# A two-layer hybrid diffusion step on one Trainium2 core: long convolution by channel halves, modulation items moved, another opening order, filler multiplications around the norms

## What is computed

```python
def trunk_layer(x, cond, p, rope, ctx_k, ctx_v):
    mod = (jax.nn.silu(cond) @ p['mod_w'] + p['mod_b']).reshape(-1, 1, 6 * D)
    sh1, sc1, g1, sh2, sc2, g2 = jnp.split(mod, 6, axis=-1)
    h = rms_norm(x, p['norm1_w']) * (1 + sc1) + sh1
    proj = h @ p['w_in']
    ...
    filt = hyena_filters(L, ...)
    ya = hyena_mixer(hy, p['hy_short_w'], p['hy_short_b'], filt, p['hy_bias'])
    ...
    yb = blocked_gqa(q, keys, vals)
    ...
    merged = (jax.nn.sigmoid(ga) * (ya @ p['w_br_a']) + jax.nn.sigmoid(gb) * (yb @ p['w_br_b'])
              + jax.nn.sigmoid(gc) * (yc @ p['w_br_c']))
    x = x + g1 * (merged @ p['w_o'])
    h2 = rms_norm(x, p['norm2_w']) * (1 + sc2) + sh2
    x = x + g2 * expert_choice_moe(h2, p['router_w'], ...)

def hyena_mixer(hy, short_w, short_b, filt, bias):
    parts = jnp.split(conv3_centred(hy, short_w, short_b), 3, axis=-1)
    z = parts[0]
    for o in range(2):                       # 512 channels, two long convolutions in turn
        z = parts[o + 1] * bidir_fftconv(z, filt[:, 0, o], filt[:, 1, o], bias[o])
    return z
```

## Time and profile before

| | us |
|---|---|
| median of 3 runs | 2371.03 (2369.81 to 2376.42) |
| the profiled execution, its device time | 2374.17 |
| the profiled execution, its span | 2372.5 |
| opening, to the first chunk at full pace | 0 to 206 |
| long convolution, layer 0 | 671.9 to 766.2 |
| long convolution, layer 1 | 1770.7 to 1855.1 |
| second norm and router, layer 0 | 915.8 to 936.5 |
| choice of tokens, layer 0 | 936.5 to 971.1 |

### The profile page before, as it was taken

One profiled execution on the slowest core, in us unless ns is written; L12 is line 12 of the kernel. 1 busy time (PEld: TensorE's weight loads), 2 busy tenths in 40 slices (PEclk: granted clock), 3 DMA queues, 4 the chain that ended last, 5 costly groups with the idle time before them and its releaser, 6 DMA issues.

```text
span 2372.5 us, 38587 instructions
## 1 busy us (share of the span) xinstructions
PE 2204.2 (93%) x14538; PEld 1859.6 (78%) x14538; DVE 1389.1 (59%) x2253; ACT 998.8 (42%) x1780; POOL 167.9 (7%) x221
## 2 busy tenths in 40 slices
PE   7998999999888998699997999999897999599999
PEld 3447999999645996588886999999763898388887
DVE  4756533611766654788887443431358764688887
ACT  2333222222631223588885321222360222488885
POOL 0000000010100100111110000001100110011110
PEclk8999999999999998799998999999998999799999
DMA  9792222233324431899992222233401341599995
GB/s 367 281 335 80 76 85 72 110 119 116 131 114 159 161 103 65 317 383 388 382 389 80 72 78 83 81 122 120 166 22 44 126 136 54 210 387 388 384 377 190
DMA packets 72959, 436.19 MB, mean 184 GB/s; under 512 B 9289, under 2 KB 9929, under 8 KB 31930
## 3 DMA queue, kind: packets, MB, share of 16 engines
q1 hardware_dynamic: 46368, 331.89, 36.5%
q0 software_dynamic: 21728, 86.51, 11.3%
q10 hardware_dynamic: 4732, 16.00, 1.9%
HBM read 384.87 MB, written 49.50 MB: 183 GB/s over the span
## 4 chain that ended last, share of the span: by engine, by line
PE 83%; DVE 8%; ACT 3%; issue 2%; DMA 2%; DVEq 2%; ACTq 0%; POOLq 0%
PE ps L610 39%; PE ps L1046 8%; PE ps L1076 7%; PE ps L1034 5%; PE ps L1050 4%; PE ps L785 4%; PE ps L907 2%; PE ps L704 2%; PE ps L835 1%; PE ps L644 1%; PE ps L921 1%; PE ps L924 1%; PE ps L686 1%; PE ps L992 1%; DVE nb L1816 1%
## 5 line engine op out<-in xcount | busy, mean ns | idle before, releaser
L610 PE MATMUL ps<-front_r 128*128 128x320 f32 x5888 | 934.8, 312 | 27.8 <-DVE front_r L1545 13.5
L610 PEld LDWEIGHTS ps<-front_r 128*128 128x128 f32 x5888 | 885.4, 189 | 34.7 <-issue 13.8
L1529 DVE TENSOR_TENSOR front_r<-ring,front_r 128x1024 fp32r<-128x1024 f32 x148 | 181.1, 1224 | 474.1 <-ACT front_r L1141 472.9
L1141 ACT ACTIVATE front_r<-ring 128x1024 fp32r<-128x1024 f32 (+1 forms) x180 | 176.4, 980 | 375.1 <-PE ps L610 291.8
L1141 ACT ACTIVATE back<-ps 128x480 f32<-128x480 f32 (+5 forms) x240 | 113.1, 496 | 423.6 <-PE ps L610 165.7
L1046 PE MATMUL ps<-back_r 128*80 128x256 f32 x640 | 171.8, 291 | 0.0
L1046 PE MATMUL ps<-back_r,front_r 128*80 128x256 f32 x640 | 164.2, 279 | 0.0
L1984 DVE TENSOR_TENSOR back_r<-front,back_r 128x512 fp32r<-128x512 f32 x208 | 137.8, 688 | 26.8 <-ACT back_r L1141 23.4
L1076 PE MATMUL ps<-back_r,front_r 128*80 128x512 f32 x576 | 149.6, 395 | 0.0
L610 PE MATMUL ps<-back_r,front_r 128*128 128x320 f32 x640 | 148.1, 313 | 0.0
L1141 ACT ACTIVATE back_r<-front 128x512 fp32r<-128x512 f32 x208 | 126.3, 637 | 12.5 <-PE ps L1050 6.5
(11 more groups left out here) (240 smaller groups left out, 3145.7 us busy)
## 6 DMA issues: line engine op xcount, KB each, us to landing
ring<-in_stream SPq DMA_DIRECT2D x186, 1024.0 KB, 7.7
front<-in_stream SPq DMA_DIRECT2D x80, 1024.0 KB, 13.5
back<-in_stream SPq DMA_DIRECT2D x48, 1024.0 KB, 14.6
gates<-back POOLq DMA_DIRECT2D x48, 320.0 KB, 2.4
back<-gates POOLq DMA_DIRECT2D x48, 320.0 KB, 3.3
kspec<-back POOLq DMA_DIRECT2D x20, 512.0 KB, 7.3
front<-kspec POOLq DMA_DIRECT2D x4, 2048.0 KB, 11.6
rows<-front ACTq DMA_DIRECT2D x10, 520.0 KB, 3.3
```

The lines of the kernel that those rows point to most:

```text
L610: mm = pe.matmul(tokh(b)[:, c0:c1], w(wp)[:, k, :], src(hp, k)[:, c0:c1], start=first, stop=last)
L1141: return act.activation(o, i, ACT.Copy)
L1529: dve.tensor_tensor(half_dst(u, 1), src, half_dst(u, 0).bitcast(F32), ALU.subtract).then_inc(w_lo, 1)
```

## The change

- **Convolution by halves of the channels.** Block 0 of the forward transform is done for channels 0 to 255 and then for 256 to 511 (`forward_first`), each half into two PSUM banks. ACT copies each half, DVE forms sum, difference and four products for each half, and combines both halves together. Block 1 (`forward_second`) is as before. The semaphore counts follow.
- **Late modulation items.** Of the twelve, two now stand in each of the two passes of layer 0, four at the choice of tokens of layer 0 (three before the transposed places, one behind), and two in each of the two passes of layer 1. `place` and `mod_place` move the items in the stream accordingly.
- **Opening.** SP waits for `network_loaded` ahead of its second item. The tables `cft` and the second decay table are issued by POOL behind `X` and no longer by ACT. PE does three modulation items ahead of the steps instead of six, and two items in each of steps 0 to 2. `magnitude` runs on half a decay table at a time.
- **Experts' first items.** SP loads item 3 of the first twelve behind items 4 and 5, in both layers.
- **Constants multiplied around norms.** `keep_busy` multiplies `ident` by `csi` (256 columns) into a free PSUM bank: 5, 1 and 4 times around the second norm of each layer, 4 and 6 times around the first norm of layer 1.

```diff
 def place(l, p):
-    return EARLY + l * ITEMS + p + (LATE if l or p >= P_BR else 0)
+    return EARLY + l * (ITEMS + 2 * GROUP) + p + (GROUP if p >= P_BR else 0) + (GROUP if not l and p >= P_EXP else 0)
...
         def step_mods(n):
+            if n < 3:
+                return 3 + 2 * n, 4 + 2 * n
             return (6 + n,) if n < 10 else (2 * n - 4, 2 * n - 3)
...
+                    if g == 1:
+                        sp.wait_ge(lay_net, 32)
                     load(g)
-                for x in range(LAP):
+                for x in (0, 1, 2, 4, 5, 3, *range(6, LAP)):
...
             pool.dma_start(X[:], a["x"]).then_inc(x_in, 16)
+            for i in range(2):
+                pool.dma_start(cft[:, i], a["cft"][:, i]).then_inc(cft_in, 16)
+            pool.dma_start(dec[1], a["decay"][1]).then_inc(dec_in, 16)
...
+            def keep_busy(bank, n):
+                for _ in range(n):
+                    pe.matmul(ps[:, bank, 0:2 * P], ident[:], csi[:].rearrange("p r n -> p (r n)"), start=True, stop=True)
...
-            for i in range(2, 6):
-                modulation(i)
-                warm(1)
+            modulation(2)
+            warm(1)
...
                     mean_squares(l, 0)
+                    keep_busy(1, 4)
                     spread(l, 0)
+                    keep_busy(1, 6)
...
+                    def forward_first(half):
+                        c0 = 256 * half
                         for odd in range(2):
+                            if half == 0:
+                                wait_tokens(odd)
                             for r in range(2):
                                 for t in range(2):
+                                    mm = pe.matmul(ps[:, 2 * half + odd, 256 * r:256 * r + 256],
+                                                   CSF[:, r, 2 * odd + t, 0:P],
+                                                   u_tm[:, 1 + 2 * odd + t, c0:c0 + 256], start=t == 0, stop=t == 1)
+                        mm.then_inc(y_fwd, 1)
...
-                    forward(0)
-                    forward(1)
-                    if l == 0:
-                        for i in range(i0, i0 + LATE // 2):
+                    forward_first(0)
+                    forward_first(1)
+                    forward_second()
+                    pe.wait_ge(y_odd, l * 6 + 3 * o + 3)
+                    for i in conv_mods(l, o):
+                        mod_rows(i)
...
+                pe.wait_ge(mg_read, l * MG + 24 + 5)
+                keep_busy(1, 5)
                 mean_squares(l, 1)
+                keep_busy(1, 1)
                 spread(l, 1)
+                keep_busy(1, 4)
...
+                if l == 0:
+                    for i in CHOICE_MODS[:-1]:
+                        mod_rows(i)
+                        if i > CHOICE_MODS[0]:
+                            mod_columns(i - 1)
+                    mod_columns(CHOICE_MODS[-2])
                 pe.wait_ge(r_places, l + 1)
                 pe.transpose(ps[0:SLOTS, 0, 0:NE], places[:], ident[0:NE, 0:NE]).then_inc(r_placesT, 1)
+                if l == 0:
+                    mod_rows(CHOICE_MODS[-1])
+                    mod_columns(CHOICE_MODS[-1])
...
+                    def products(kt, c0, c1):
                         for i in range(2):
                             for j in range(2):
+                                dve.tensor_tensor(ymul[:, 2 * i + j, :, c0:c1], ysum[:, i, :, c0:c1],
+                                                  Kb[:, kt, i, j, c0:c1].unsqueeze(1).to_broadcast([P, 2, c1 - c0]), ALU.mult)
...
+                    for half in range(2):
+                        dve.wait_ge(y_odd, l * 6 + 3 * o + half + 1)
+                        dve.tensor_tensor(ysum[:, 0, :, c0:c1], even, odd, ALU.add)
+                        ins = dve.tensor_tensor(ysum[:, 1, :, c0:c1], even, odd, ALU.subtract)
+                        products(0, c0, c1)
+                    combine(0)
```

More of the change, by code:

```diff
@@ L95, in homes @@
     for g in range(STREAM):
-        x = (g - MODS) % ITEMS - P_EXP if g >= MODS + P_BR else -1
+        x = g - place(int(g >= place(1, 0)), P_EXP)
         slot = x % LAP if x >= 0 and x % LAP >= SLOT else g % SLOT
@@ L1220, in _ @@
             act.activation(fh1, farg, ACT.Sin).then_inc(f_sin, 1)
-            for i in range(1, 5):
-                mod_copy(i)
+            mod_copy(1)
+            mod_copy(2)
             act.wait_ge(f_arg, 2)
@@ L1441, in _ @@
                 store_rows(4)
+                if l == 0:
+                    for i in CHOICE_MODS:
+                        mod_copy(i)
+                        if i > CHOICE_MODS[0]:
+                            late_add(i - 1)
+                    late_add(CHOICE_MODS[-1])
                 def evac_rows(n):
@@ L1657, in _ @@
             dve.wait_ge(filt_in, 48)
-            magnitude(0)
-            for i in range(1, 5):
-                mod_add(i)
+            magnitude(0, 0)
+            mod_add(1)
             for n in range(20):
@@ L1869, in _ @@
                         dve.tensor_tensor(Yb[:, kt, 1], ysum[:, 0], ysum[:, 1], ALU.subtract).then_inc(y_mul, 1)
-                    settle()
-                    dve.wait_ge(y_fwd, l * 6 + 3 * o + 3)
+                    for half in range(2):
+                        c0, c1 = 256 * half, 256 * half + 256
+                        settle()
+                        dve.wait_ge(y_odd, l * 6 + 3 * o + half + 1)
+                        even = ps[:, 2 * half, :].rearrange("p (r n) -> p r n", r=2)
+                        odd = yodd[0].rearrange("p r n -> p (r n)")[:, DH * half:DH * half + DH]\
+                            .rearrange("p (r n) -> p r n", r=2)
+                        dve.tensor_tensor(ysum[:, 0, :, c0:c1], even, odd, ALU.add)
+                        ins = dve.tensor_tensor(ysum[:, 1, :, c0:c1], even, odd, ALU.subtract)
+                        if half:
+                            ins.then_inc(y_sum, 1)
+                        settle()
+                        products(0, c0, c1)
+                    combine(0)
+                    settle()
+                    dve.wait_ge(y_odd, l * 6 + 3 * o + 3)
+                    even = ps[:, 4:6, :]
+                    dve.tensor_tensor(ysum[:, 0], even, yodd[1], ALU.add)
+                    dve.tensor_tensor(ysum[:, 1], even, yodd[1], ALU.subtract).then_inc(y_sum, 1)
+                    settle()
+                    products(1, 0, DH)
+                    combine(1)
+                    settle()
+                    dve.wait_ge(y_fwd, l * 8 + 4 * o + 4)
                     for i in range(2):
```

101 lines of the change are left out of this document (52 added, 49 removed).

## The result

| | before | after |
|---|---|---|
| median, us | 2375.78 (5 runs, 2369.81 to 2377.66) | 2360.52 (5 runs, 2356.64 to 2364.74) |
| ratio to before | | 0.9937, 95% interval 0.9923 to 0.995 |
| profiled execution, device time | 2374.17 | 2359.76 |
| its span | 2372.5 | 2358.1 |

What follows compares the result with a forecast made beforehand. TensorE, busy 93% of the span, was the bound, leaving its waits and low-clock stretches to win. Terms -17.2-7.6+1.0+0.9-8.5 = -31.4 us gave 2342.8 from the profiled 2374.17, 2340 for the median; range 2331 to 2355.

Steps and rivals of the forecast that it cites:

- The opening: Start to layer 0's convolution: first taps some 17 us sooner, but the stream's bytes bind, so -8.5 us.
- the stream eats the opening: Rival, chance 0.12: DMA engines full from 43 to 57 us, a waiting item blocks TensorE's queue, no opening gain, 2348.5.
- The convolution: Both layers' convolutions: halves and fewer modulation items give -3.7 us in layer 1, -13.5 in layer 0, together -17.2.
- pass 0: First convolution pass: VectorE starts at about T0+4.4, 3.8 us sooner; the pass falls from 41.91 to 38.2 us, gaining 3.7.
- my 0.6: Splitting block 0 into halves: six more instruction pairs with one more drain cost VectorE 0.6 us.
- Pass 1: Second convolution pass: VectorE waits 3.6 us for the spectrum, halves gain nothing; left at 42.5 us, bounds -1 and +1.
- The second norm: Both layers: fillers hold the clock, spread 1.2 us less, router 8.6 in place of 11.2; -3.8 each, -7.6 in all.
- The first norm of layer 1: Four fillers between sum of squares and spread, where the clock is already low: +1.0 us, from -0.2 to +2.7.
- the choice: Choice of tokens: three items fit PE's wait, the fourth delays expert item 3's load; +0.9 us in layer 0, nothing in layer 1.
- Slower by a clock that falls in the dense stretches: Rival, chance 0.03: granted clock falls in projections and experts; a fall of 0.025 costs 46 us and gives 2386.

Runs made afterwards that it cites:

- e11: The changed kernel without SP's wait ahead of its second item, all else of the opening as changed: 2357.2 us, 0.9921.
- e4: The changed kernel with the second network layer, its argument and sines ahead of modulation item 1: 2354.04 us, 0.9912.
- e12: The changed kernel with `warm(6)` in place of `warm(1)` behind `modulation(2)`, in TensorE's idle time ahead of the first taps: 2354.61 us, 0.9905.
- e7: The kernel of e6 with tokens `X` issued after six items are used and the first norm's squares three steps later: 2351.36 us, 0.9904.
- e5: The changed kernel with POOL loading block 0's part of pass 1's spectrum a step sooner, the rest later: 2350.1 us, 0.9897.
- e10: The kernel of e2 (block 0 whole) with the early spectrum load of e5: 2364.33 us, 0.996.
- e2: The changed kernel with block 0 of the forward transform whole, as before, two items kept in each pass: 2363.21 us, 0.9955.
- e6: The kernel of e4 with POOL issuing the second decay table, `sel`, `onesm`, `rope` and `csi` only after eleven items are used: 2352.4 us, 0.9895.
- e3: The changed kernel without the multiplications of constants (`keep_busy` issues none): 2364.82 us, 0.9954.
- e8: The changed kernel with 7, 2, 5 constants around the second norm and 8, 2, 6 around layer 1's first norm: 2355.57 us, 0.9913.
- e9: The changed kernel with the edits of e4 to e8 together, and POOL's drains ahead of its loads: 2341.28 us, 0.9864.

## Why the prediction was half right

**The opening (-8.5, measured +0.4) is the step that failed.** It put the gain into one number, "8.5 us however early the taps start", from bytes: 17.1 MB at 420 GB/s from 2 us on. That sum gives item 8 at 42.7 us; it was used at 53.18, and no item was waited for in the steps. So the bytes were not the bound; the chain to the taps and TensorE's own work, part of it at the lower clock, were. Three things were wrong with the sum.

- The order on TensorE was not followed, nor what SP's wait does to item 1. I took the chain to the taps to lose 5 us at the inputs and 11 at the items moved behind it, and forecast the first taps at 25 to 28 us. They came at 34.65. The 11 us were 8.3: from the second network layer to the taps PE takes 8.15 us in place of 16.45 (22.61 to 30.76, before 23.00 to 39.45). The 5 us were 3.7 at the first layer and 0.4 at the second. `network(1)` stands behind `modulation(1)` on PE, and the same wait that lets the inputs through first makes item 1 land at 18.83, where it had landed by 8.9 without it (e11). Moving `network(1)` ahead of the item had the taps at 27.72 (e4). That order of calls stands in both kernels, and the prediction's sum never placed them in a row.
- The clock was not priced. The wait of 4.67 us that the shorter chain left ahead of the taps goes over into a stretch at 0.50, and the steps pay for it, 3.0 us at the first spectrum (e12).
- The rate was too high. The windows of 6 us up to 42 us give 15.1 MB, not 16.8. From 6 to 12 us the engines are full at only 251 GB/s. It isn't the small inputs: from 8 to 12 us it is 207 GB/s, and nearly all of it is ACT's queue with 59 packets of 13 KB on average (the rows at e11). And the bytes bound only once the first point was mended (e4), where moving unneeded ones away gave up to 5.7 us at the first spectrum (e7).

The rival "the stream eats the opening" had the right number (no gain), but not for its reason.

**The convolution (-17.2, measured -13.5).** The mechanism was right in its main parts: DVE at 4.36 of pass 0, the landing from `kspec` in pass 1, and the 9.8 us by which layer 0 was longer than layer 1 are gone (82.38 against 82.74). Sizes: pass 0 gained 3.2, not 3.7. A first half and its twin took 7.89 us on DVE where the whole block took 7.15, so splitting cost 0.7, near my 0.6. The estimate of 0.94, from the rule (N+151)/0.96 ns on the Trainium skill's page "VectorE: DVE Perf Modes", section "The TRN2 errata — SBUF-src ops pay a fixed extra latency per instruction", is 0.2 above what was measured. Pass 1 was left "at its 42.5" and was 1.4 to 1.6 us longer than the 41.77 before, most of it by the clock: its tokens took 3.78 us in place of 3.40, and the inverse behind them, which started low, 11.4 to 11.8 in place of 10.52. The bound there was +1 for the instructions, and the items' clock was not in it. What I took as a neutral replacement, a wait that takes the place of another, was worth 9 us (e5, with the halves; without them nothing, e10): I had priced the wait and not asked what removing it costs, one DMA split in two.

**The second norm (-7.6, measured -5.9).** I said that with the fillers "no gap is over 0.8 us" and so the spread would halve. In layer 0 it stayed at 2.47, and the clock is 0.50 from 909.9 to 913.0. What stands ahead is 0.78 us of idleness, ten one-column multiplications, and one filler. The low stretch shrank from about 10 us to 3, which gave the router its 8.77. In other executions of the same code the spread takes 1.35 in layer 0 (e2, e4, e5, e6, e10) and 2.47 in layer 1 (e7, e11, e12). The Trainium skill's page "TensorE: Matmul & The Clock Gate", section "What's actually happening", says that the point at which the clock rises behind a kernel's start varies from run to run. That is about the rise; in these traces the fall in mid-kernel varies too, by 1.1 us a norm.

**The first norm of layer 1 (+1.0, measured +1.5) and the choice (+0.9, measured +1.5).** The constants do cost 1.4 us at the norm, as forecast in kind, but the 1.5 at the convolution stands without them too (e3), so its agreement with the forecast is luck. Constants ahead of the sum give back 1.6 at the norm (e8, e9). The choice took 1.3 us more in layer 0 (34.55 to 35.84) and 0.2 in layer 1; the 0.9 had no row behind it, and no run takes its items apart.

**Slower by a clock that falls in the dense stretches** did not happen: 0.99 in the experts, before and after.

## What to carry to other kernels

Before counting bytes or engine time for an opening, write down for each call on the chain what stands ahead of it in its own engine's queue: an item that nobody on the chain needs can hold it for 8 us. When one queue's loads are held back so that others land sooner, write down when the held ones land too; here that was 10 us later. When a gain ends at a new wait, price the removal of that wait as well; here it was worth 4.4 us a layer, more than the 3.2 that the halves gave with the wait left in. And a stretch of idle TensorE cost twice here, once as the wait and again in what ran at the lower clock behind it.

## What the runs showed of the hardware

- **Identical code, different lengths.** From its start to the last inverse, pass 1 with items takes 43.1 to 43.7 us in most executions, but 40.64 (e7), 40.96 (e8), 41.25 (e11) in layer 0 and 41.42 (e12) in layer 1. With no wait on the spectrum it is 38.8 in all four cases (e5, e9). The experts of layer 1 to the end take 311.3 to 314.6 us over the runs, which covers the 1.5 us of "all else" in the table. So in this kernel a pass with 3 us of idle TensorE in it has such a spread of its own, and a single trace may show either end.
- **A transfer that is issued later than another queue's can find the engines taken.** Item 1 (1 MB) was issued at 7.12, behind 2 MB of ACT's, and took 11.71 us, in which all queues together moved 3.65 MB. Issued at 1.33, ahead of them, it had landed by 8.92 (e11). The Trainium skill's page "DMA: Bandwidth & Descriptors", section "Queues, rings and completion order", says that each DMA engine takes turns between its queues. The trace of the change agrees from 12 to 18 us, where SP's queue moved 1.38 MB and ACT's 0.85. It doesn't from 8 to 12, where SP's moved 0.03 and ACT's 0.79 with items 1 to 3 issued; why SP's queue stood still is not shown.
- **A drain on POOL waits for the DMAs that it issued.** In e7 and in e6 the next store went out 1.3 us after the last landing (67.67 and 69.01, 69.11 and 70.44); with the drains ahead of the loads (e9) at 60.34, while the last load landed at 66.89.
